# Two modulation chunks summed on TensorE, the first weights loaded earlier, and two blocks alternated by halves of the features

## The chip, the cores and the metric

One core of one Trainium2 chip. The metric is the device time in microseconds of one execution of the whole kernel, the median of the runs shown. Everything is float32; large matmuls are made of three float32r products.

## The reference, cut to what matters

A vector `c` of 1024 numbers gives a shift, a scale and a gate for each of the 1024 features; the normalized input (256 tokens by 1024 features) is scaled and shifted, and then multiplied by a wide input matrix, whose column blocks feed four attention branches a to d. A second, longer part of the model follows, which the change does not touch.

```python
mod = (jax.nn.silu(c) @ w_ada + b_ada)[:, None, :]
shift, scale, gate = jnp.split(mod, 3, axis=-1)
h = rms_norm(x, norm_g) * (1.0 + scale) + shift
(a_q, a_kv, a_g, a_z, b_q, b_k, b_v, b_z,
 c_q, c_k, c_v, c_z, d_q, d_k, d_v, d_z) = jnp.split(h @ w_in, IN_OFFSETS, axis=-1)
...
y_d = retention(heads(d_q), heads(d_k), heads(d_v))
...
yi = y.reshape(B, S, BRANCH_W) * jax.nn.silu(z)
term = jax.nn.sigmoid(h @ w_merge[i]) * (yi @ w_br[i])
...
return x + gate * (merged @ w_out)
```

## The kernel before

Each engine runs a program written out by hand, in its own order; an engine that waits for a semaphore holds up all that stands behind it on that engine.

**The stream of weights.** `weight_plan` (L105) lists all weights as chunks of 4 feature tiles (512 features) by up to 512 columns, 1 MB each. SyncE loads them in this order into four raw buffers (`sp_program`, L3004); chunk i may start when chunk i-4 is told `("weights low", i-4)`, which means that its raw form has been read for the last time. Two kinds of chunk come in this stream:

- Chunks of matrices that are multiplied. ScalarE rounds the chunk to its high part (`act_split`, L509), VectorE subtracts (`vec_split`, L519) to get the low part, and `pe_block` (L580) multiplies high and low parts. There are three pairs of buffers for the parts. I call these chunks split 0, 1, 2 and so on. A step of `pe_block` over 512 features is 48 matmuls of 256 columns where features are the output (`d_qk`, `c_qk`), 24 of 512 columns where tokens are (`pe_columns`: `d_vz`, `c_vz`).
- Chunks of `w_ada`, which gives the modulation. `vec_modulation` (L533 and L535) multiplies each of the 4 feature tiles by a number per partition and sums them on VectorE. For scale and shift, `pe_columns_of` (L829) then sums over the partitions with 4 matmuls of one column (8 matmul records in the profile), and `vec_first_columns` (L895 to L898) adds the bias. The gate's four chunks are each summed by `vec_split`, right behind the low part of the chunk that precedes them in the plan (L535).

**The start.** The plan begins with scale and shift of features 0 to 511 ("half 0"), then scale of half 1, then the first `w_in` chunk (`d_qk`, features 0 to 511), then shift of half 1, then the second `d_qk` chunk, then a gate chunk and `d_vz`. PE transposes the scaled x (`pe_turn_x`, L840), ScalarE applies scale and shift (L864) and rounds to the high operand (L868), VectorE makes the low operand (L906). Operand half n is ready when the last of these has run. `d_qk` step 0 needs half 0, step 1 needs half 1. The shift columns of half 1 are summed over the partitions within `d_qk` step 0, behind its 28th matmul, and operand half 1 is made after that.

**Later.** The blocks run on PE in the order `d_qk`, `d_vz`, `c_qk`, `c_vz`, `b_qk`, `b_vz`, `a_vz`, `a_qk`, and the small work of the four branches is put between their steps by `interleave`, by how many chunks each engine has passed. At split 11, branch d's retention output is normalized: VectorE (L1187 to L1195), GpSimd (L674, L676), VectorE again (L1198, L1028), and then PE transposes the result (L1036).

Of the kernel before, what the change touches and what calls it, by code (L numbers as in the profile page):

```python
# [14 lines left out]
P = 128  # L15
# [89 lines left out]
def weight_plan(w):  # L105
# [17 lines left out]
    first_in, shift = chunks(w_in, KT, [(W_D_Q, 512)]), modulation(ada, "shift", 1)  # L123
    plan.extend(modulation(ada, "scale", 0) + modulation(ada, "shift", 0) + modulation(ada, "scale", 1) + first_in[:1] + shift + first_in[1:])
    gate = modulation(ada, "gate", 0) + modulation(ada, "gate", 1)
    for block in ((W_D_V, 512), (W_C_Q, 512), (W_C_V, 512)):
        plan.append(gate.pop(0))
        add(w_in, [block])
    plan.append(gate.pop(0))
    add(w_in, [(W_B_Q, 384)], [(W_B_V, 384)])  # L130
    add(w_in, [(W_A_KV + 3 * HD, HD), (W_A_KV + 5 * HD, HD + 3 * NH + BW)], [(W_A_Q, BW + 3 * HD), (W_A_KV + 4 * HD, HD)])
    for i in ORDER:
# [358 lines left out]


def chain(*gens):
    for g in gens:
        yield from g
# [16 lines left out]

def vec_split(k, n, gate=True):

    if n < len(k.split):
        i, j = k.split[n], n % k.N_SPLIT
        raw, high, low = (chunk_view(k, t, i) for t in (k.w_raw[i % k.N_RAW], k.w_high[j], k.w_low[j]))
        k.vec.wait_ge(("weights high", i), ("weights", i), ("multiplied", n - k.N_SPLIT) if n >= k.N_SPLIT else None)
        k.vec.eng.tensor_tensor(low, raw, high.bitcast(F32), ALU.subtract).then_inc(*k.vec.tells("weights_low", ("weights low", i)))  # L519
        if gate and i + 1 < len(k.plan) and k.plan[i + 1][2] and k.plan[i + 1][2][0] == "gate":  # L520
            vec_modulation(k, *k.plan[i + 1][2])


def vec_modulation(k, name, n, first):

    V, i = k.vec, k.whole_weights[name, n, first]
    raw, total = chunk_view(k, k.w_raw[i % k.N_RAW], i), k.sums_of[name][:, n * CN:(n + 1) * CN]
    V.wait_ge("c silu", ("weights", i), "gate bias" if name == "gate" else None)
    for j in range(CK):
        number = k.c_silu[:, first + j:first + j + 1]  # L530
        V.wait_ge(V.last)
        if first + j == 0 and name != "gate":
            V.eng.tensor_scalar(total, raw[:, j, :], number, None, ALU.mult).then_inc(*V.tells("modulations"))  # L533
        else:
            V.eng.scalar_tensor_tensor(total, raw[:, j, :], number, total, ALU.mult, ALU.add).then_inc(  # L535
                *V.tells("modulations", (name, n), ("weights low", i)))


def act_chunk(k):

    i = k.act.chunk
    k.act.chunk += 1
    act_split(k, i + k.N_SPLIT - 1)


def vec_chunk(k):
    i = k.vec.chunk
    k.vec.chunk += 1
    vec_split(k, i + k.N_SPLIT - 1)

# [269 lines left out]


def pe_columns_of(k, name, n):

    key, at = ("columns", n), CK * ("scale", "shift").index(name)
    bank = k.product.take(key)
    k.pe.wait_ge((name, n), "common", None if at else k.product.before(key))
    for j in range(CK):
        c = (CK * n + j) * P
        mm = k.pe.eng.matmul(bank[:, at + j:at + j + 1], k.sums_of[name][:, c:c + P], k.ones[:, 0:1], start=at + j == 0, stop=True, skip_group_check=True)  # L829
    mm.then_inc(*k.pe.tells("columns", key))  # L830


# [11 lines left out]
def pe_condition(k):  # L844
    pe, tr = k.pe, k.pe.eng.transpose
    pe.wait_ge("common", "c row")
    tr(k.small.take("c")[:, 0:KT], k.c_row[:, :], k.ident[0:KT, 0:KT]).then_inc(*pe.tells("turned", "c turned"))
    pe.wait_ge("condition rows")
    tr(k.small.take("condition")[:, 0:3 * KT], k.cond_rows[:, :], k.ident[0:3 * KT, 0:3 * KT]).then_inc(*pe.tells("turned", "condition turned"))
    pe_columns_of(k, "scale", 0)  # L850
    pe_columns_of(k, "shift", 0)
    for n in range(2):
        pe_turn_x(k, n)
    pe_columns_of(k, "scale", 1)
    pe.ended("condition")


def act_first_half(k, n):
    A, columns = k.act, k.stat(("columns", n), 2 * CK)
    for b in range(2):  # L860
        for j in range(2):
            f = 2 * b + j
# [3 lines left out]
        at = slice(CK * n + 2 * b, CK * n + 2 * b + 2)  # L866
        A.wait_ge(A.last)
        A.eng.activation(k.H_first.high[:, at, :], k.whole[:, 2 * b:2 * b + 2, :], ACT.Copy).then_inc(*A.tells("operand_high", ("first high", n, b)))  # L868


def act_condition(k):
# [11 lines left out]
    act_first_half(k, 0)  # L883
    act_split(k, 1)
    act_first_half(k, 1)
    A.ended("condition")
# [3 lines left out]
def vec_first_columns(k, n):  # L890
    V, columns, ps = k.vec, k.stat(("columns", n), 2 * CK), k.product.of(("columns", n))
# [4 lines left out]
    V.eng.tensor_tensor(columns[:, CK:2 * CK], ps[:, CK:2 * CK], bias, ALU.add).then_inc(*V.tells("vec_steps", k.product.free(("columns", n))))  # L896
# [13 lines left out]
def vec_condition(k):  # L910
# [18 lines left out]
    V.ended("condition")  # L929
# [693 lines left out]
def act_branches(k):  # L1623
# [27 lines left out]
    def fill():  # L1651
        yield from act_qk(k, "d_qk", k.q_d, k.k_d, "d_qk")
        yield from act_vz(k, "d_vz", k.v_d, k.z["d"])
        yield from act_qk(k, "c_qk", k.q_c, k.k_c, "c_qk")
# [21 lines left out]
def vec_branches(k):  # L1676
# [3 lines left out]
    def fill():  # L1680
        yield from vec_chunks(k, 2)
        yield from vec_vz(k, "d_vz", BW, k.z["d"])
        yield from vec_chunks(k, 2)
# [1389 lines left out]
```

## Time and profile before

| | |
|---|---|
| median of 3 runs | 1157.37 us (1156.54 to 1158.16) |
| the profiled execution's own time | 1156.71 us |
| its span, first to last instruction | 1155.2 us |
| PE busy | 1116.3 us (97%) |
| DVE busy (VectorE) | 769.3 us (67%) |
| ACT busy (ScalarE) | 582.8 us (50%) |
| mean granted TensorE clock | 0.992 |
| first matmul of `d_qk` | 32.49 us |
| last matmul of `d_vz` ends, branch work begins | 63.14 us |

The span is 1.5 us shorter than the time of its own execution. PE is busy nearly everywhere but in the first 32 us, so what matters is when its first block starts, and how long PE waits after that. A granted clock of 1.00 in the profile is 2.4 GHz, 0.50 is 1.2 GHz.

### The profile page before, as it was taken

Reading aid. Unit: us, or ns where it says so; the run is one execution under the profiler, and the core shown is the slowest. Engines: PE = TensorE matmul, PEld = TensorE weight load, DVE = VectorE, ACT = ScalarE, POOL = GpSimd, SP = SyncE. Lnnn points to the kernel's source line nnn. Section 1 sums busy time; section 2 is a strip of 40 time slices with the busy share of each in tenths; the row PEclk is TensorE's granted clock in tenths of the full one; section 3 lists DMA queues with packets and bytes.
Section 4 is the critical chain, followed back from the end, with each engine's and each line's share of the span. In section 5 each row is a group of like instructions: output and inputs, shape, how many; then the busy total and the mean of one; then the engine's idle time right before and its main releaser. Section 6 shows DMA issues by size and latency. Waiting matters only on the chain.

```text
span 1155.2 us, 15556 instructions
## 1 busy us (share of the span) xinstructions
PE 1116.3 (97%) x6395; PEld 976.4 (85%) x6395; DVE 769.3 (67%) x1022; ACT 582.8 (50%) x830; POOL 49.3 (4%) x82
## 2 busy tenths in 40 slices
PE   2899999999999999999999999999999999999997
PEld 2789988888889987898988888788888989888886
DVE  6866655665787996745588765456876545788642
ACT  2547664444464764654544544446765545444441
POOL 3021000000010000000100000000011000000000
PEclk9999998999999999999999999999999999999999
DMA  9895343465546403543655555555345436555450
GB/s 350 307 315 167 114 144 128 158 224 165 195 141 204 140 1 109 186 143 123 175 182 180 185 184 180 189 181 176 111 157 171 146 109 201 177 189 182 152 176 37
DMA packets 105879, 195.10 MB, mean 169 GB/s; under 512 B 6105, under 2 KB 22641, under 8 KB 105808
## 3 DMA queue, kind: packets, MB, share of 16 engines
q1 hardware_dynamic: 103248, 187.51, 48.5%
q0 software_dynamic: 2560, 6.60, 2.1%
q8 instruction: 50, 0.82, 0.3%
q14 instruction: 21, 0.17, 0.0%
HBM read 193.04 MB, written 1.05 MB: 168 GB/s over the span
## 4 chain that ended last, share of the span: by engine, by line
PE 88%; DVE 4%; ACT 4%; DMA 2%; issue 1%; POOL 1%; SPq 0%; DVEq 0%; ACTq 0%; POOLq 0%
PE product L580 59%; PE product L614 5%; PE small L614 5%; PE small L2325 4%; PE product L616 3%; PE small L616 3%; ACT w_high L509 1%; DMA w_raw<-in_w_ada 1%; PE small L724 1%; PE small L1903 1%; PE small L1275 1%; DVE w_low L519 1%; DMA w_raw<-in_w_in 1%; PE small L1286 1%; PE small L1924 1%
## 5 line engine op out<-in xcount | busy, mean ns | idle before, releaser
L519 DVE TENSOR_TENSOR w_low<-w_raw,w_high 128x2048 fp32r<-128x2048 f32 (+3 forms) x172 | 377.6, 2198 | 219.6 <-ACT w_high L509 217.9
L509 ACT ACTIVATE w_high<-w_raw 128x2048 fp32r<-128x2048 f32 (+3 forms) x172 | 315.4, 1837 | 198.6 <-PE product L580 142.0
L580 PE MATMUL product<-w_high,H 128*128 128x512 f32 (+2 forms) x768 | 244.0, 392 | 0.2 <-DVE w_low L519 0.2
L580 PE MATMUL product<-H,w_high 128*128 128x256 f32 x1136 | 214.3, 288 | 5.6 <-DVE H L906 4.6
L580 PEld LDWEIGHTS product<-H,w_high 128*128 128x128 f32 x1136 | 181.8, 195 | 7.2 <-issue 6.3
L580 PEld LDWEIGHTS product<-w_high,H 128*128 128x128 f32 x768 | 144.8, 189 | 29.6 <-issue 1.2
L580 PE MATMUL product<-H,w_low 128*128 128x256 f32 x568 | 163.0, 287 | 0.0
L580 PE MATMUL product<-w_low,H 128*128 128x512 f32 (+2 forms) x384 | 149.3, 389 | 0.0
L580 PEld LDWEIGHTS product<-H,w_low 128*128 128x128 f32 x568 | 110.7, 195 | 0.3
L614 PE MATMUL product<-H,w_high 128*128 128x512 f32 x256 | 90.8, 399 | 0.0
L614 PE MATMUL small<-H,w_high 128*128 128x512 f32 x256 | 90.8, 399 | 0.0
L580 PEld LDWEIGHTS product<-w_low,H 128*128 128x128 f32 x384 | 72.8, 189 | 13.3 <-issue 0.2
L616 PE MATMUL product<-H,w_low 128*128 128x256 f32 x256 | 71.9, 281 | 0.0
L616 PE MATMUL small<-H,w_low 128*128 128x256 f32 x256 | 71.9, 281 | 0.0
L580 PE MATMUL product<-w_high,hidden_low 128*128 128x512 f32 x176 | 69.5, 395 | 0.0
L580 PE MATMUL product<-w_low,hidden_high 128*128 128x512 f32 x176 | 69.4, 395 | 0.0
L580 PE MATMUL product<-w_high,hidden_high 128*128 128x512 f32 x176 | 69.4, 395 | 0.0
L2482 DVE SCALAR_TENSOR_TENSOR conv_out<-conv_in,taps,conv_out 128x256 f32<-128x256 f32 x147 | 58.8, 489 | 0.0
L614 PEld LDWEIGHTS small<-H,w_high 128*128 128x128 f32 x256 | 48.1, 188 | 12.1
L614 PEld LDWEIGHTS product<-H,w_high 128*128 128x128 f32 x256 | 48.1, 188 | 12.0
L616 PEld LDWEIGHTS product<-H,w_low 128*128 128x128 f32 x256 | 48.4, 189 | 0.0
L616 PEld LDWEIGHTS small<-H,w_low 128*128 128x128 f32 x256 | 48.4, 189 | 0.0
(385 smaller groups left out, 1634.8 us busy)
## 6 DMA issues: line engine op xcount, KB each, us to landing
w_raw<-in_ffn_w_gate SPq DMA_DIRECT2D x20, 1024.0 KB, 5.1
w_raw<-in_ffn_w_up SPq DMA_DIRECT2D x20, 1024.0 KB, 5.2
w_raw<-in_ffn_w_down SPq DMA_DIRECT2D x20, 1024.0 KB, 5.1
w_raw<-in_w_merge SPq DMA_DIRECT2D x16, 1024.0 KB, 5.1
w_raw<-in_w_ada SPq DMA_DIRECT2D x12, 1024.0 KB, 7.9
w_raw<-in_w_in SPq DMA_DIRECT2D x8, 1024.0 KB, 6.3
w_raw<-in_mem_w_k SPq DMA_DIRECT2D x8, 1024.0 KB, 5.1
w_raw<-in_conv_w_pw SPq DMA_DIRECT2D x16, 512.0 KB, 4.7
```

Source lines behind the costliest of these rows:

```text
L509: k.act.eng.activation(chunk_view(k, k.w_high[j], i), chunk_view(k, k.w_raw[i % k.N_RAW], i), ACT.Copy).then_inc(*k.act.tells("weights_hig ...
L519: k.vec.eng.tensor_tensor(low, raw, high.bitcast(F32), ALU.subtract).then_inc(*k.vec.tells("weights_low", ("weights low", i)))
L580: mm = pe.eng.matmul(bank[:, off:off + wide], a, r, start=b not in started, stop=True, skip_group_check=True)
L614: pe.eng.matmul(bank[:, :].rearrange("p (i n) -> p i n", n=S), high[:, j, column], x.parts[:, :, first + j, :], start=first + j == 0, stop ...
L616: mm = pe.eng.matmul(bank[:, 0:S], low[:, j, column], x.high[:, first + j, :], start=False, stop=True, skip_group_check=True)
L724: tr = k.pe.eng.transpose(bank[:, j * S + t * P:j * S + (t + 1) * P], k.X[:, t, c:c + P], k.ident)
L1275: mm = pe.eng.matmul(scores[:, i * nk:(i + 1) * nk], q[:, h, t * P:(t + 1) * P], kk_of(h)[:, 0:nk], start=i == 0, stop=True, skip_group_ch ...
L1286: mm = pe.eng.matmul(mixed[:, i * HD:(i + 1) * HD], p[:, b * P:(b + 1) * P], v_of(h, j), start=b == 0, stop=True, skip_group_check=True)
L1903: mm = pe.eng.matmul(bank[:, t * S:(t + 1) * S], k.q_mem[:, kt, t * P:(t + 1) * P], k.mem_keys[:, kt, :], start=t == 0 and j == 0, stop=Tr ...
L1924: mm = pe.eng.matmul(bank[:, f * S:(f + 1) * S], k.mem_values[:, j, c:c + P], p[:, j * S:(j + 1) * S], start=f == 0 and j == 0, stop=True, ...
L2325: mm = pe.eng.matmul(bank[:, 0:S], slot[:, i, :], k.conv_in[:, f, tap:tap + S], start=tap in (0, VEC_TAPS) and i == 0, stop=tap == TAPS - 1)
L2482: V.eng.scalar_tensor_tensor(y[:, f, :], src, wt, y[:, f, :], ALU.mult, ALU.add).then_inc(*V.tells("taps_vec", ("conv out", f)))
```

## The change

The plan's head is put in another order. Before, with the splits numbered: scale 0, shift 0 (two chunks each), scale 1 (two), `d_qk` (split 0), shift 1 (two), `d_qk` (1), gate, `d_vz` (2, 3), gate, `c_qk` (4, 5), gate, `c_vz` (6, 7), gate, `b_qk` (8, 9), `b_vz` (10, 11), `a_vz` (12, 13). After: scale 0, shift 0, `d_qk` (0), scale 1 (two), `d_vz` (1), shift 1 (first), `d_qk` (2), shift 1 (second), `d_vz` (3), `c_qk` (4, 5), gate, `c_vz` (6, 7), `b_qk` (8), gate, `b_qk` (9), `b_vz` (10, 11), gate, `a_vz` (12, 13), gate.

The first chunk of scale 1 and the second of shift 1 are no longer summed by VectorE: `pe_direct_columns` multiplies the raw weights by `c_silu` on PE, 16 matmuls of one column each. The columns of half 1 go to another PSUM ring. VectorE takes one of the two pairs of tiles of half 1 from ScalarE (`vec_last_whole`). `d_qk` and `d_vz` alternate: step 0 of each, then step 1 of each; the columns of scale 1 are summed within `d_qk` step 0, those of shift 1 within `d_vz` step 0.

```diff
-    plan.extend(modulation(ada, "scale", 0) + modulation(ada, "shift", 0) + modulation(ada, "scale", 1) + first_in[:1] + shift + first_in[1:])
+    plan.extend(modulation(ada, "scale", 0) + modulation(ada, "shift", 0) + first_in[:1] + modulation(ada, "scale", 1))
...
+    plan.extend(d_vz[:1] + shift[:1] + first_in[1:] + shift[1:])
+    a_vz = chunks(w_in, KT, [(W_A_KV + 3 * HD, HD), (W_A_KV + 5 * HD, HD + 3 * NH + BW)])
+    for part in (d_vz[1:] + c_qk, c_vz + b_qk[:1], b_qk[1:] + b_vz, a_vz):
+        plan.extend(part + [gate.pop(0)])
...
+def alternate(*gens):
+
+    gens = list(gens)
+    while gens:
+        for gen in list(gens):
+            said = next(gen, "end")
...
+            if said == "end":
+                gens.remove(gen)
+            else:
+                yield said
...
+DIRECT = [("scale", 1, 0), ("shift", 1, CK)]
+
+
+def columns_ring(k, n):
+    return k.small if n else k.product
...
+def pe_direct_columns(k, name, n, first):
+
+    key, at, ring, i = ("columns", n), CK * ("scale", "shift").index(name), columns_ring(k, n), k.whole_weights[name, n, first]
+    raw, bank = chunk_view(k, k.w_raw[i % k.N_RAW], i), ring.take(key)
+    k.pe.wait_ge("c silu", ("weights", i), None if at else ring.before(key))
+    for f in range(CK):
+        for j in range(CK):
+            mm = k.pe.eng.matmul(bank[:, at + f:at + f + 1], raw[:, j, f * P:(f + 1) * P], k.c_silu[:, first + j:first + j + 1],
+                                 start=(at, f, j) == (0, 0, 0), stop=True, skip_group_check=True)
+    mm.then_inc(*k.pe.tells("columns", key, ("weights low", i)))
...
     pe_columns_of(k, "scale", 0)
+    pe_turn_x(k, 0)
     pe_columns_of(k, "shift", 0)
-    for n in range(2):
-        pe_turn_x(k, n)
-    pe_columns_of(k, "scale", 1)
+    pe_turn_x(k, 1)
+    pe_direct_columns(k, "scale", 1, 0)
     pe.ended("condition")
...
+def vec_last_whole(k):
+
+    V, columns, key = k.vec, k.stat(("columns", 1), 2 * CK), ("x", 1, 1)
+    V.wait_ge(V.last, ("x turned", 1, 1))
+    for j in range(2):
+        f = 2 + j
+        V.eng.tensor_scalar(k.whole[:, f, :], k.small.of(key)[:, S * j:S * (j + 1)], columns[:, f:f + 1], columns[:, CK + f:CK + f + 1],
+                            ALU.mult, ALU.add).then_inc(*V.tells("last_whole", "last whole", k.small.free(key)))
...
-    vec_modulation(k, "scale", 1, 0)
     vec_first_columns(k, 0)
-    vec_modulation(k, "scale", 1, CK)
     vec_split(k, 0)
     vec_first_low(k, 0)
-    for first in range(0, KT, CK):
-        vec_modulation(k, "shift", 1, first)
+    vec_modulation(k, "scale", 1, CK)
+    vec_split(k, 1)
+    vec_modulation(k, "shift", 1, 0)
+    vec_split(k, 2)
     vec_first_columns(k, 1)
-    vec_split(k, 1, False)
+    vec_last_whole(k)
     vec_first_low(k, 1)
-    vec_modulation(k, "gate", 0, 0)
...
+    def last_columns():
+        pe_direct_columns(k, "shift", 1, CK)
+        pe_columns_of(k, "shift", 1)
+
     def fill():
-        yield from pe_block(k, "d_qk", k.H_first, KT, FEATURES, inside={(0, 28): lambda: pe_columns_of(k, "shift", 1)})
-        yield from pe_columns(k, "d_vz", k.H_first, KT)
+        yield from alternate(pe_block(k, "d_qk", k.H_first, KT, FEATURES, inside={(0, 28): lambda: pe_columns_of(k, "scale", 1)}),
+                             pe_columns(k, "d_vz", k.H_first, KT, inside={(0, 10): last_columns}))
```

## Rows read from the trace of the kernel before

**Rows 1.** The page: busy time of each engine, and the granted clock in 40 slices:

```profile
PE 1116.3 (97%) x6395; PEld 976.4 (85%) x6395; DVE 769.3 (67%) x1022; ACT 582.8 (50%) x830; POOL 49.3 (4%) x82
...
PEclk9999998999999999999999999999999999999999
```

**Rows 2.** Windows: length, then each engine's busy time, PEclk, DMA share, GB/s:

```profile
32.49:63.14 30.65, 28.21 (x152) 25.58 (x152) 25.16 (x27) 14.94 (x15) 1.13 (x2) 0.94 0.90 307
...
110.94:1150.00 1039.06, 1031.48 (x5891) 898.66 (x5891) 691.82 (x922) 527.82 (x758) 26.19 (x44) 1.00 0.47 157
```

**Rows 3.** Waits of PE: waited for, us in total, times, longest:

```profile
PE product L829 <- DVE gain L535: 12.4, 3, 6.1
...
PE product L580 <- DVE H L906: 4.6, 2, 2.3
...
PE small L1036 <- DVE y L1028: 0.9, 1, 0.9
```

**Rows 4.** Timeline of PE: start, us, line, operation, idle before and its releaser:

```profile
21.54 1.87 PE L829 MATMUL product<-common,gain 128*128 128x1 f32 x8 [6.14 <-DVE gain L535]
...
23.27 3.65 PE L840 MATMUL small<-common,scaled_x 128*128 128x128 f32 x16
...
32.49 0.55 PE L580 MATMUL product<-H,w_high 128*128 128x256 f32 x1 [2.35 <-DVE H L906]
...
38.58 1.05 PE L829 MATMUL product<-common,gain 128*128 128x1 f32 x8
...
44.40 0.36 PE L580 MATMUL product<-H,w_high 128*128 128x256 f32 x1 [2.27 <-DVE H L906]
...
52.04 0.50 PE L580 MATMUL product<-w_high,H 128*128 128x512 f32 x1 [0.16 <-DVE w_low L519]
```

**Rows 5.** Windows of PE alone: length, busy (instructions), granted clock, DMA:

```profile
32.49:38.41 5.92, 5.92 (x28) 1.00 0.96 330
...
38.41:42.00 3.59, 3.59 (x30) 1.00 0.99 322
...
45.24:48.65 3.41, 3.41 (x18) 0.50 0.51 188
```

**Rows 6.** SyncE's queue at 10 and 18 us: issues, and us to landing:

```profile
10.29 0.37 SPq L3014 DMA_DIRECT2D w_raw<-in_w_ada  x1
...
w_raw<-in_w_ada SPq DMA_DIRECT2D x1, 1024.0 KB, 10.6
...
w_raw<-in_w_in SPq DMA_DIRECT2D x1, 1024.0 KB, 8.3
```

**Rows 7.** Timelines of ScalarE and VectorE around the first operand half:

```profile
28.38 1.00 ACT L864 ACTIVATE whole<-small,stats 128x256 f32<-128x256 f32 x2
...
29.42 0.63 ACT L868 ACTIVATE H<-whole 128x512 fp32r<-128x512 f32 x1
...
28.51 2.29 DVE L519 TENSOR_TENSOR w_low<-w_raw,w_high 128x2048 fp32r<-128x2048 f32 x1 [0.28 <-ACT w_high L509]
...
31.66 0.69 DVE L906 TENSOR_TENSOR H<-whole,H 128x512 fp32r<-128x512 f32 x1 [0.26 <-ACT H L868]
```

**Rows 8.** PE at 185 us, timeline, then the window behind it:

```profile
184.79 3.70 PE L1380 MATMUL small<-cmp_t,cmp_w 128*128 128x16 f32 x32
...
188.60:191.04 2.44, 2.44 (x8) 0.50 0.25 93
```

**Rows 9.** Timelines of VectorE and PE where branch d's output is turned:

```profile
75.23 3.11 DVE L535 SCALAR_TENSOR_TENSOR gate<-w_raw,stats,gate 128x512 f32<-128x512 f32 x4
...
105.60 1.75 DVE L519 TENSOR_TENSOR w_low<-w_raw,w_high 128x1536 fp32r<-128x1536 f32 x1
...
107.73 0.55 DVE L1256 TENSOR_TENSOR merged<-merged,small 128x384 f32<-128x384 f32 x1
...
109.46 0.69 DVE L1198 TENSOR_TENSOR y<-y,stats 128x512 f32<-128x512 f32 x1 [1.18 <-POOL stats L676]
...
110.94 0.66 PE L1036 MATMUL small<-common,y 128*128 128x128 f32 x4 [0.88 <-DVE y L1028]
```

More of the change, by code:

```diff
@@ L123, in weight_plan @@
     first_in, shift = chunks(w_in, KT, [(W_D_Q, 512)]), modulation(ada, "shift", 1)
-    plan.extend(modulation(ada, "scale", 0) + modulation(ada, "shift", 0) + modulation(ada, "scale", 1) + first_in[:1] + shift + first_in[1:])
+    plan.extend(modulation(ada, "scale", 0) + modulation(ada, "shift", 0) + first_in[:1] + modulation(ada, "scale", 1))
     gate = modulation(ada, "gate", 0) + modulation(ada, "gate", 1)
[L126 to L131, printed above, removed]
+    d_vz, c_qk, c_vz, b_qk, b_vz = (chunks(w_in, KT, [block]) for block in ((W_D_V, 512), (W_C_Q, 512), (W_C_V, 512), (W_B_Q, 384), (W_B_V, 384)))
+    plan.extend(d_vz[:1] + shift[:1] + first_in[1:] + shift[1:])
+    a_vz = chunks(w_in, KT, [(W_A_KV + 3 * HD, HD), (W_A_KV + 5 * HD, HD + 3 * NH + BW)])
+    for part in (d_vz[1:] + c_qk, c_vz + b_qk[:1], b_qk[1:] + b_vz, a_vz):
+        plan.extend(part + [gate.pop(0)])
+    add(w_in, [(W_A_Q, BW + 3 * HD), (W_A_KV + 4 * HD, HD)])
     for i in ORDER:
@@ L490, in drain @@
         pass
+def alternate(*gens):
[3 more added lines that the diff above has]
+            said = next(gen, "end")
+            while said == "piece":
+                yield said
+                said = next(gen, "end")
+            if said == "end":
+                gens.remove(gen)
+            else:
+                yield said
 def chain(*gens):
@@ L510, in act_split, with vec_split @@
             *k.act.tells("weights_high", ("weights high", i)))
-def vec_split(k, n, gate=True):
+def vec_split(k, n):
     if n < len(k.split):
@@ L519, in vec_split @@
         k.vec.eng.tensor_tensor(low, raw, high.bitcast(F32), ALU.subtract).then_inc(*k.vec.tells("weights_low", ("weights low", i)))
-        if gate and i + 1 < len(k.plan) and k.plan[i + 1][2] and k.plan[i + 1][2][0] == "gate":
+        if i + 1 < len(k.plan) and k.plan[i + 1][2] and k.plan[i + 1][2][0] == "gate":
             vec_modulation(k, *k.plan[i + 1][2])
@@ L531, in vec_modulation @@
         V.wait_ge(V.last)
-        if first + j == 0 and name != "gate":
+        if j == 0 and name != "gate" and (first == 0 or (name, n, 0) in DIRECT):
             V.eng.tensor_scalar(total, raw[:, j, :], number, None, ALU.mult).then_inc(*V.tells("modulations"))
@@ L542, in act_chunk @@
     k.act.chunk += 1
-    act_split(k, i + k.N_SPLIT - 1)
+    if i:
+        act_split(k, i + k.N_SPLIT - 1)
 def vec_chunk(k):
@@ L548, in vec_chunk @@
     k.vec.chunk += 1
-    vec_split(k, i + k.N_SPLIT - 1)
+    if i:
+        vec_split(k, i + k.N_SPLIT - 1)
 def pe_block(k, key, x, tiles, items, order=None, inside={}, early={}):
@@ L819, in pool_condition @@
     g.wait_ge(*k.all_ended("condition"))
+DIRECT = [("scale", 1, 0), ("shift", 1, CK)]
+def columns_ring(k, n):
+    return k.small if n else k.product
 def pe_columns_of(k, name, n):
-    key, at = ("columns", n), CK * ("scale", "shift").index(name)
-    bank = k.product.take(key)
-    k.pe.wait_ge((name, n), "common", None if at else k.product.before(key))
+    key, at, ring = ("columns", n), CK * ("scale", "shift").index(name), columns_ring(k, n)
+    bank = ring.take(key)
+    k.pe.wait_ge((name, n), "common", None if at else ring.before(key))
     for j in range(CK):
         c = (CK * n + j) * P
-        mm = k.pe.eng.matmul(bank[:, at + j:at + j + 1], k.sums_of[name][:, c:c + P], k.ones[:, 0:1], start=at + j == 0, stop=True, skip_group_check=True)
+        mm = k.pe.eng.matmul(bank[:, at + j:at + j + 1], k.sums_of[name][:, c:c + P], k.ones[:, 0:1], start=(at, j, n) == (0, 0, 0), stop=True,
+                             skip_group_check=True)
     mm.then_inc(*k.pe.tells("columns", key))
+def pe_direct_columns(k, name, n, first):
[7 more added lines that the diff above has]
+    mm.then_inc(*k.pe.tells("columns", key, ("weights low", i)))
 def pe_turn_x(k, n):
@@ L860, in act_first_half @@
     for b in range(2):
-        for j in range(2):
+        for j in range(0 if n and b else 2):
             f = 2 * b + j
@@ L866, in act_first_half @@
         at = slice(CK * n + 2 * b, CK * n + 2 * b + 2)
-        A.wait_ge(A.last)
+        A.wait_ge("last whole" if n and b else A.last)
         A.eng.activation(k.H_first.high[:, at, :], k.whole[:, 2 * b:2 * b + 2, :], ACT.Copy).then_inc(*A.tells("operand_high", ("first high", n, b)))
@@ L884, in act_condition @@
     act_split(k, 1)
+    act_split(k, 2)
     act_first_half(k, 1)
@@ L890, in vec_first_columns @@
 def vec_first_columns(k, n):
-    V, columns, ps = k.vec, k.stat(("columns", n), 2 * CK), k.product.of(("columns", n))
+    V, columns, ring = k.vec, k.stat(("columns", n), 2 * CK), columns_ring(k, n)
+    ps = ring.of(("columns", n))
     at = slice(CK * n, CK * (n + 1))
@@ L895, in vec_first_columns @@
     V.eng.tensor_tensor(columns[:, 0:CK], ps[:, 0:CK], scale, ALU.add).then_inc(*V.tells("vec_steps"))
-    V.eng.tensor_tensor(columns[:, CK:2 * CK], ps[:, CK:2 * CK], bias, ALU.add).then_inc(*V.tells("vec_steps", k.product.free(("columns", n))))
+    V.eng.tensor_tensor(columns[:, CK:2 * CK], ps[:, CK:2 * CK], bias, ALU.add).then_inc(*V.tells("vec_steps", ring.free(("columns", n))))
     V.wait_ge(V.last)
     V.eng.scalar_tensor_tensor(columns[:, 0:CK], columns[:, 0:CK], 1.0, gain, ALU.add, ALU.mult).then_inc(*V.tells("columns_copied", ("columns copied", n)))
+def vec_last_whole(k):
[5 more added lines that the diff above has]
+                            ALU.mult, ALU.add).then_inc(*V.tells("last_whole", "last whole", k.small.free(key)))
 def vec_first_low(k, n):
@@ L1651, in fill @@
     def fill():
-        yield from act_qk(k, "d_qk", k.q_d, k.k_d, "d_qk")
-        yield from act_vz(k, "d_vz", k.v_d, k.z["d"])
+        yield from alternate(act_qk(k, "d_qk", k.q_d, k.k_d, "d_qk"), act_vz(k, "d_vz", k.v_d, k.z["d"]))
         yield from act_qk(k, "c_qk", k.q_c, k.k_c, "c_qk")
@@ L1680, in fill @@
     def fill():
-        yield from vec_chunks(k, 2)
-        yield from vec_vz(k, "d_vz", BW, k.z["d"])
+        yield from alternate(vec_chunks(k, 2), vec_vz(k, "d_vz", BW, k.z["d"]))
         yield from vec_chunks(k, 2)
```

## The prediction

> **What bounds the kernel now.** I read the page first. PE is busy for 1116.3 of 1155.2 us, and the granted clock is near 1.00 in all slices but one [rows 1]. The windows and the table of PE's waits then tell where PE is not busy. Of its 39 us of idle time, 24 fall before the first matmul of `d_qk` at 32.49 us; behind 110.94 us it is busy for 1031.48 of 1039.06 us [rows 2, 3]. So the rest of the kernel is bound by PE, and a shift of PE near the start reaches the end unchanged. Two waits lie where the change works: `d_qk` step 1 waits 2.27 us for the low operand of half 1, and at 110 us PE waits 0.88 us for branch d's gated output [rows 3, 4, 9].
>
> PE's clock matters too. From 32.49 to 38.41 us PE issued 28 matmuls of 256 columns in 5.92 us, 0.211 us each: that is 1.2 GHz, although the row says 1.00. From 38.41 us on, 30 matmuls (among them the 8 short ones of the columns) took 3.59 us, the pace of 2.4 GHz [rows 5]. Before the lower stretch PE had transposed and made one-column matmuls. 0.84 us after the wait of 2.27 us the granted clock fell to 0.50 for 3.41 us, in which PE did half its work: such a fall costs 1.7 us [rows 4, 5].
>
> **The change, part by part.**
>
> *Start of `d_qk`.* The first `w_in` chunk goes from place seven of the stream to place five. It takes over the place of a chunk issued at 10.29 us that landed 10.6 us later, at 20.9 us; before, it was issued at 18.3 and landed at 26.6 [rows 6]. ScalarE is free then, so its high part (1.9 us) is made by 22.8 us. The shift columns of half 0 are summed at 21.54 us as before, and end at 23.4 us [rows 4]. Their three small vector steps end near 24.0 us. ScalarE then makes operand half 0: 1.0 + 0.6 + 1.0 + 0.6 us with overlap is 3.25 us, to 27.3 us; the last low part takes 0.7 us, to 28.05 us [rows 7]. VectorE's split 0 (2.29 us) fits beside it, 24.1 to 26.4 us. The data of `d_qk` are thus ready 4.4 us earlier than at 32.49 us.
>
> But PE is not. Behind the shift columns stand 8 transposes (half of 3.65 us, to 25.1 us), and then `pe_direct_columns` for scale 1: 16 float32 matmuls, 32 records. The same form, 128x128 weights by one column, took 1.87 us for 8 records at this stage, with 1.73 us from its start to the next instruction, so 0.216 us a record [rows 4]. 32 records are 6.9 us, at most 7.5. `d_qk` starts at about 25.15 + 6.9 = 32.05 us, against 32.49: a gain of 0.4 us, and at worst a loss of 0.1. The earlier landing is nearly all eaten by PE's own queue.
>
> *`d_qk` and `d_vz`.* The matmuls are the same in number: 96 of 256 columns and 48 of 512. Added is the second direct sum (shift 1), now at the full clock. Its price is in the trace: 32 records with 128x128 weights and 16 columns took 3.70 us [rows 8]; with the change of work around it I take 3.75. Before, one sum over partitions (8 records, 0.96 us from start to start) ran within `d_qk` and one stood ahead of it, while data were missing; now both stand within: 0.96 us more [rows 4]. Removed is the wait of 2.27 us and the 0.16 us before `d_vz` [rows 4].
>
> Is operand half 1 in time? With these durations `d_qk` step 0 ends at 41.75 us, 10 matmuls of `d_vz` at 0.227 us reach 44.1, the direct sum 47.9, the columns 48.85 us. From there the vector steps take 0.45 us, ScalarE's first pair and its high part 1.7 us, the second high part 0.65 us (VectorE has made that pair meanwhile), the low part 0.7 us: ready at about 52.4 us, 3.55 us later [rows 7]. What hides it is the 14 matmuls of `d_vz` left: 3.2 us at 2.4 GHz, about 5 where the clock falls. I take no wait; without the fall it is 0.4 us. The weights are no limit: split 1 is ready at 33.5 us, split 2 at 41.6, split 3 (ScalarE and VectorE come to it when half 1 is done) at 56.8 against a need at 59.4. `d_qk`'s heads, now copied by ScalarE behind step 2 instead of step 1, are done near 62, before the scores at 65.
>
> *The clock there.* The fall of 3.41 us behind the wait goes with the wait. In its place stand 40 records of one column, 4.7 us. The 32 records of 16 columns at 184.79 us were followed by a fall at 188.60 us to 0.50 [rows 8]. I take one fall again, so no difference.
>
> The Trainium skill (TensorE: Matmul & The Clock Gate, Part 1) says that activity releases the throttle, which the row of 38.41 us agrees with; it would let PE's unbroken work from 21.5 us on count. By it the first block would start warm, which is the third rival below; [rows 4, 5] speak against it, as 5.4 us of columns and transposes without a gap did not bring the upper level.
>
> Sum of this part: -0.4 - 2.4 + 3.75 + 0.96 = **+1.9 us** at the end of `d_vz`, 65.0 us instead of 63.14.
>
> *VectorE and the gate chunks.* The two chunks taken off VectorE (about 3 us each) were under PE's other work or under data that are no longer waited for: nothing further. The gate's four sums of 3.11 us stood behind operand half 1 and splits 3, 5 and 7; they now stand behind splits 5, 8, 11 and 13 [rows 9]. Behind 5, 8 and 13 VectorE has idle time or its readers have slack. Split 11 is the row at 105.60 us [rows 9]. Behind it stand two steps of branch c (to 108.3 us), then 1.18 us of idle time for GpSimd's root, then L1198 at 109.46 us and L1028, and PE's transposes at 110.94 us wait for the latter. With 3.11 us put behind split 11, the two steps of branch c end at 111.4 us, and L1198 starts 3.11 - 1.18 = 1.93 us later; with one handover between instructions, 2.0. PE's wait grows from 0.88 to 2.9 us: **+2.0 us**. What waits behind it on PE is `b_vz`'s second step, and all of the rest. ScalarE's part of branch c moves by 3.2 us, of which 2.0 are PE's own, and split 12 is then ready 3.8 us before its need; no second wait. Lower bound 0, if VectorE is further ahead than before; upper bound 3.1, the whole sum.
>
> *The clock there.* Around that wait PE has 1.6 us of short matmuls before it and 0.4 us of transposes behind it, 4.9 us in all without large matmuls. Before, the same place with 0.88 us of wait kept 1.00. The 2.27 us wait in front of `d_qk` step 1 brought a fall [rows 4, 5]. The cost is 0 or 1.7 us. The new wait is nearer to the second row, but where in time it comes is open: I put in **+0.9 us**.
>
> **Sum.** 1.9 + 2.0 + 0.9 = 4.8 us. Against the profiled execution's own 1156.71 us (1.5 us more than its span) that is 1161.5; its time is 0.66 us under the median of 1157.37 us, to which I add the sum: **1162.2 us**.
>
> **Rivals.**
> 1. *The gate sum behind split 11 is hidden.* VectorE has two modulation sums less to do, and could be ahead of its times of before. Against it: at 105 us its work is chained to PE through ScalarE and not to its load at 50 us. Only the first 1.9 us remain: 1159.3 us.
> 2. *The direct sums cost more.* 0.234 us a record at the start (+0.6), a wait of 0.4 for half 1, and the full fall behind the second wait, or a longer one (the fall at 188.60 lasted beyond 191 us, as short matmuls followed [rows 8]): +1.7 more on the 4.8, 1165 us or above.
> 3. *Not slower: the direct sum holds the clock up.* PE has no gap from 21.5 us on. If the clock reaches its upper level half-way through the first direct sum, the rest of it takes 1.9 us instead of 3.6 (-1.7), the first 28 matmuls 3.4 instead of 6.1 us (-2.7), and no fall comes within `d_vz` (-1.7, less 0.5 of waiting for half 1). 1.9 - 5.6 = -3.7 us for the start; with the wait at 110 us 1155.7, without it 1153.7 us. It decides once the first matmuls of `d_qk` are 0.12 us apart. For it: PE works without a break. Against it: [rows 8], where the same form let the clock fall.
> 4. *It comes out even.* The early landing and the removed wait together weigh the direct sums, because the clock's stretches fall otherwise: 1157.4 us.
>
> **Chances.** Forecast (both waits as worked out, 1160.5 to 1164.0 us) 0.50; rival 1 0.17; rival 2 0.10; rival 3 0.16; rival 4 0.07. 0.2% is 2.3 us, about what a measurement of this kernel tells from no change. Slower by more than that, above 1159.7: the forecast, rival 2 and part of rival 1, 0.62. Faster, below 1155.1: half of rival 3 and a little more, 0.12. Same: the rest, 0.26. The range for 8 in 10 goes from 1155.3 us, with part of rival 3 in it, to 1165.0 us.
>
> **What would show it.** Right: the first `w_in` chunk lands near 21 us; 32 records of the direct sum from 25 to 32 us, right in front of the first L580 matmul, which waits for no operand; no wait for H in `d_qk` step 1; another 32 records in about 3.7 us near 44 us, with a stretch of granted clock 0.50 behind them; `d_vz` ends near 65 us; PE's wait for L1028 is near 2.9 us. Wrong: a direct record of 0.12 us at the start; `d_qk` starting near 28 to 30 us; the L1028 wait unchanged; or a new wait of PE for `w_low`, `queries_keys` or a DMA.

## The result and the profile after

| | before | changed |
|---|---|---|
| median | 1157.76 us (1156.54 to 1159.50, 4 runs) | 1163.67 us (1161.92 to 1164.43, 4 runs) |
| ratio | | 1.0047 (95% interval 1.0034 to 1.0060) |
| span of the profiled execution | 1155.2 us | 1160.6 us |

By the medians the change made the kernel 5.9 us slower, by the ratio 5.4 us, with an interval from 3.9 to 7.0 us. Forecast were 4.8 us (1162.2 us against 1157.4) and a range of 1155.3 to 1165.0 us.

The start first. This is the timeline of PE in the changed kernel, to be held against [rows 4]:

```profile
21.55 1.87 PE L853 MATMUL product<-common,gain 128*128 128x1 f32 x8 [1.11 <-DVE gain L550]
...
23.28 1.95 PE L877 MATMUL small<-common,scaled_x 128*128 128x128 f32 x8
...
25.21 6.96 PE L865 MATMUL small<-stats,w_raw 128*128 128x1 f32 x32
...
32.04 0.56 PE L597 MATMUL product<-H,w_high 128*128 128x256 f32 x1
...
37.89 0.95 PE L853 MATMUL small<-common,gain 128*128 128x1 f32 x8
...
43.46 3.62 PE L865 MATMUL small<-stats,w_raw 128*128 128x1 f32 x32
...
46.95 1.11 PE L853 MATMUL small<-common,gain 128*128 128x1 f32 x8
...
52.72 0.28 PE L597 MATMUL product<-H,w_high 128*128 128x256 f32 x1
...
64.03 0.70 PE L1051 MATMUL small<-queries_keys 64*128 64x256 f32 x2
```

The 32 records of the first direct sum stand from 25.21 to 32.04 us, right in front of the first matmul of `d_qk`, and that matmul has no idle time before it: it waits for PE itself. It starts 0.45 us earlier than before. The operand it needs was there long ago, as ScalarE and then VectorE show (timelines of both, against [rows 7]):

```profile
20.90 1.91 ACT L524 ACTIVATE w_high<-w_raw 128x2048 fp32r<-128x2048 f32 x1 [2.49 <-DMA w_raw<-in_w_in]
...
26.67 0.63 ACT L905 ACTIVATE H<-whole 128x512 fp32r<-128x512 f32 x1
```

```profile
27.33 0.69 DVE L955 TENSOR_TENSOR H<-whole,H 128x512 fp32r<-128x512 f32 x1 [0.57 <-ACT H L905]
```

The first `w_in` chunk's high part begins at 20.90 us, and the last low part of half 0 ends at 28.0 us. PE came 4.0 us later. Further down in PE's timeline, the second direct sum takes 3.49 us from its start to the next instruction (43.46 to 46.95) and the columns 0.97 us; `d_qk` step 1 (52.72) does not wait; branch work begins at 64.03 us against 63.14.

Now the place at 110 us, VectorE above and PE below, against [rows 9]:

```profile
106.49 1.75 DVE L534 TENSOR_TENSOR w_low<-w_raw,w_high 128x1536 fp32r<-128x1536 f32 x1
...
108.35 3.14 DVE L550 SCALAR_TENSOR_TENSOR gate<-w_raw,stats,gate 128x512 f32<-128x512 f32 x4
...
111.41 0.55 DVE L1308 TENSOR_TENSOR merged<-merged,first_constants 128x384 f32<-128x384 f32 x1
...
113.19 0.69 DVE L1076 TENSOR_TENSOR y<-y,z_d 128x512 f32<-128x512 f32 x1
```

```profile
112.02 0.43 PE L1059 MATMUL small<-v_c,merged 128*128 128x64 f32 x2 [2.53 <-DVE merged L1308]
...
112.97 1.22 PE L1051 MATMUL small<-queries_keys 64*128 64x256 f32 x2
...
114.55 1.11 PE L1084 MATMUL small<-common,y 128*128 128x128 f32 x4
```

The gate's sum stands behind split 11 (L534 at 106.49) and pushes branch c's step L1308 to 111.41 us. PE's small matmul L1059 needs that step and waits 2.53 us. Branch d's output (L1076) is ready at 113.9 us, and PE's transposes of it (L1084, at 114.55) no longer wait. So the wait is there with nearly the forecast's size, but at an earlier instruction of PE, branch c's mix, and not at branch d's transposes.

The third view is windows of PE alone (length, busy time, granted clock, DMA), laid on the stretches where the clock stood low:

```profile
32.04:37.52 5.48, 5.48 (x27) 1.00 0.78 254
...
47.76:51.18 3.42, 3.42 (x10) 0.50 0.84 264
...
112.62:119.44 6.82, 6.82 (x24) 0.50 1.01 337
```

The first 27 matmuls of `d_qk` run at the 1.2 GHz pace although the row says 1.00, as in [rows 5]. The clock falls to 0.50 behind the second direct sum for 3.4 us, and at 112.62 us, 0.6 us behind the end of the new wait, for 6.8 us. The second of these costs 3.4 us, where I had put in 0.9.

When the starts of the same PE instruction in both traces are subtracted, the changed kernel is 0.89 us late at 63.14 us and still so at 104 us, 3.6 us late at the mix behind the new wait, and 5.87 us late at the next small matmuls of branch c (115.62 us before). Between there and 890 us this does not change (5.43 us behind that). Both losses lie before 122 us, and the rest carries them to the end. The second adds up: 1.65 us more of waiting and 3.4 us of clock are 5.05 us, against 4.98 from branch work to there.

### The profile page after: what moved, and what is told of

Same layout as the page of the kernel before. It is cut to its first block, busy times and chain, and to the rows that moved or that the text cites. A ratio compares the mean times of both kernels' runs of the same rounds, so it can differ in the third digit from the quotient of the medians.

```text
span 1160.6 us, 15674 instructions
## 1 busy us (share of the span) xinstructions
PE 1128.5 (97%) x6459; PEld 988.1 (85%) x6459; DVE 764.3 (66%) x1016; ACT 581.4 (50%) x828; POOL 49.0 (4%) x82
## 3 DMA queue, kind: packets, MB, share of 16 engines
HBM read 193.04 MB, written 1.05 MB: 167 GB/s over the span
## 4 chain that ended last, share of the span: by engine, by line
PE 91%; DVE 4%; ACT 3%; DMA 1%; issue 1%; SPq 0%; POOL 0%; DVEq 0%; ACTq 0%; POOLq 0%
PE product L597 61%; PE product L631 5%; PE small L631 5%; PE small L2375 4%; PE product L633 3%; PE small L633 3%; DMA w_raw<-in_w_ada 1%; ACT w_high L524 1%; PE small L741 1%; PE small L1953 1%; PE small L865 1%; PE small L1323 1%; DVE w_low L534 1%; PE small L656 1%; PE small L1334 1%
## 5 line engine op out<-in xcount | busy, mean ns | idle before, releaser
L534 DVE TENSOR_TENSOR w_low<-w_raw,w_high 128x2048 fp32r<-128x2048 f32 (+3 forms) x172 | 377.5, 2197 | 226.8 <-ACT w_high L524 224.8
L631 PEld LDWEIGHTS product<-H,w_high 128*128 128x128 f32 x256 | 48.1, 188 | 11.9
```

Source lines behind the costliest of these rows:

```text
L631: pe.eng.matmul(bank[:, :].rearrange("p (i n) -> p i n", n=S), high[:, j, column], x.parts[:, :, first + j, :], start=first + j == 0, stop ...
```

## The experiments

The experiments were timed in three sets (1 to 4, 5 to 7, 8 and 9), each on one chip beside the kernel before, so kernels of different sets are compared by their ratios to it. Two numbers besides the median are used. **Start** is the time from PE's transposes at 23.27 us [rows 4], or what answers to them, to branch work (63.14 us before), so that a late landing of the first loads is left out: 39.9 us before. It comes from one trace of each kernel. **Lost clock** is one minus the mean granted clock, times the span, averaged over all executions of a kernel. Every execution has some: 10.3 us before on average, and 6.9 to 16.2 us in 34 executions; a single trace shows one draw.

| kernel | median, us | ratio (95%) | start | lost clock | mean time less lost clock |
|---|---|---|---|---|---|
| before | 1157.4 | | 39.9 | 10.3 | 1147.7 |
| changed | 1163.7 | 1.0047 | 40.8 | 12.5 | 1150.9 |
| changed, again | 1164.5 | 1.0049 (1.0036 to 1.0062) | 41.3 | 14.2 | 1149.9 |
| gate sums moved | 1161.2 | 1.0026 (1.0017 to 1.0035) | 41.7 | 12.9 | 1148.1 |
| before, gate sums late | 1161.3 | 1.0025 (1.0015 to 1.0035) | 37.8 | 12.3 | 1148.7 |
| shift chunk on VectorE | 1160.7 | 1.0020 (1.0011 to 1.0030) | 38.5 | 11.0 | 1149.4 |
| both | 1155.5 | 0.9983 (0.9972 to 0.9993) | 38.4 | 8.4 | 1147.7 |
| both, no direct sum | 1155.7 | 0.9980 (0.9968 to 0.9992) | 38.1 | 10.5 | 1145.1 |
| both, shift chunk first | 1156.7 | 0.9987 (0.9975 to 0.9998) | 39.3 | 9.4 | 1147.1 |
| no direct sum, shift first | 1158.3 | 1.0000 (0.9990 to 1.0010) | 39.4 | 11.9 | 1146.3 |
| direct sum spread | 1159.3 | 1.0005 (0.9993 to 1.0016) | 40.0 | 9.7 | 1149.4 |

Lost clock is not the time that the lower level costs, and the last column is not the time without it. The trace of the kernel before has its last low stretch from 1151 us on, where PE has no work left. The low pace of the first matmuls of `d_qk` is not in it either, as the row there says 1.00 [rows 5]. Over the 34 executions of the kernel before, taking the lost clock off makes the spread larger and not smaller (standard deviation 2.2 us instead of 1.35). The column is shown, but no reading below rests on it.

**Start** has a draw of its own. In the seven traces that have the first direct sum, `d_qk` began 8.75 to 8.76 us behind the start of the transposes each time, but its step 0, the same work, ended 16.8 to 17.9 us behind them, because the pace doubled sooner or later. So a difference of up to 1.1 us in start can be this alone.

### 1. The gate sums moved

```diff
-    for part in (d_vz[1:] + c_qk, c_vz + b_qk[:1], b_qk[1:] + b_vz, a_vz):
+    for part in (d_vz[1:] + c_qk, c_vz, b_qk, b_vz + a_vz):
```

> The changed kernel with one thing moved: the gate sums stand behind splits 5, 7, 9 and 13 instead of 5, 8, 11 and 13. In the traces PE ran 0.89 us later than before at the end of d_vz, and 5.87 us later behind branch d's turn at 110 us. My theory: the 3.11 us sum behind split 11 makes nearly all of the 5 us between (a longer wait of PE and the fall of the clock that it brings). Then this kernel is 4.5 to 5 us faster than the changed one, about 1158.7 us, with PE's wait there back at 0.9 us and a granted clock of 1.00 from 105 to 125 us. Rival: VectorE's chain through ScalarE and GpSimd is late in any case, and the gate sum only fills a wait; then no more than 1 us comes back.

Measured: 1161.2 us; by the ratios 2.4 us less than the changed kernel, and 2.7 less than its second timing, where 4.5 to 5 had been expected. PE's waits from 60 to 150 us, and windows of PE:

```profile
PE small L1084 <- DVE y L1076: 0.9, 1, 0.9
```

```profile
47.15:53.97 6.82, 6.82 (x22) 0.50 0.64 219
...
100.00:130.00 30.00, 29.11 (x183) 1.00 0.72 231
```

The wait is back at 0.9 us and the clock stays up from 100 to 130 us, so the mechanism at 110 us is as stated, and the rival (VectorE's chain is late in any case) is out. In this trace the whole 5 us came back: between branch work and 121.5 us PE makes up 5.0 us on the first trace of the changed kernel, and 3.4 us on its second trace. The medians show only half of the 5 us, with an uncertainty of 1.8. Part of the difference is that the fall behind the direct sum lasted 6.8 us here and not 3.4; over ten executions the lost clock is 12.9 us, no less than the changed kernel's 12.5. I had taken the clock's share from one trace as if it were fixed.

### 2. The late gate sums alone, in the kernel before

```diff
-    for block in ((W_D_V, 512), (W_C_Q, 512), (W_C_V, 512)):
-        plan.append(gate.pop(0))
...
+    for part in (d_vz + c_qk, c_vz + b_qk[:1], b_qk[1:] + b_vz, a_vz):
+        plan.extend(part + [gate.pop(0)])
...
     vec_first_low(k, 1)
-    vec_modulation(k, "gate", 0, 0)
```

> The kernel before with one part of the change alone: the gate sums behind splits 5, 8, 11 and 13. My theory: 3 to 5 us slower than before, 1161 to 1163 us, by the same wait for VectorE near 111 us and the clock behind it, while d_vz ends at 63.1 us as before or 0.2 us earlier. Rival (the start sets everything): within 1 us of before.

Measured: 1161.3 us, 3.9 us slower than before (2.9 by the ratio), as the theory says, with nothing else of the change in it. Its wait of PE, and three rows of its PE timeline:

```profile
PE small L1009 <- DVE merged L1258: 2.5, 1, 2.5
```

```profile
24.37 3.58 PE L839 MATMUL small<-common,scaled_x 128*128 128x128 f32 x16
...
29.38 1.05 PE L828 MATMUL product<-common,gain 128*128 128x1 f32 x8 [1.44 <-DVE gain L534]
...
62.16 0.70 PE L1001 MATMUL small<-queries_keys 64*128 64x256 f32 x2
```

The wait is the same 2.5 us, at the same small matmul. The start is even shorter than before by 2.1 us. In this trace the clock had reached its upper level by the columns at 29.38 us, behind nothing but short matmuls, transposes and 1.4 us of waiting (they took 1.05 us instead of 1.87), and it did not fall around the 2.28 us wait for the second operand half. It did fall at 31.2 us, within the 3.0 us wait in front of `d_qk`, for 6.8 us. The edit touches nothing there, and the lost clock over its 11 executions is 12.3 us against 10.3 before, so I take the shorter start as a draw of this one execution.

### 3. The second direct sum undone

```diff
-DIRECT = [("scale", 1, 0), ("shift", 1, CK)]
+DIRECT = [("scale", 1, 0)]
...
     vec_modulation(k, "shift", 1, 0)
+    vec_modulation(k, "shift", 1, CK)
     vec_split(k, 2)
...
     def last_columns():
-        pe_direct_columns(k, "shift", 1, CK)
         pe_columns_of(k, "shift", 1)
```

> The changed kernel with the second direct sum undone: VectorE sums the second chunk of shift 1 as before (3.1 us, ahead of split 2), PE makes only its 8 column records in d_vz step 0. My theory: PE loses 3.5 us of work and the fall of the clock behind it (1.7 us), but operand half 1, now behind VectorE's split 2, is then what d_qk step 1 waits for, 1 to 2 us; d_vz ends near 60.3 us instead of 64.0, and the kernel is 3 to 4 us faster than the changed one, about 1160 us, as the wait near 111 us stays. Rival: the direct sum was hidden behind operand half 1; then d_vz ends at 63.5 us or later and the time is that of the changed kernel.

Measured: 1160.7 us; by the ratios 3.1 us less than the changed kernel (3.4 less than its second timing). PE's timeline:

```profile
45.30 1.05 PE L853 MATMUL small<-common,gain 128*128 128x1 f32 x8 [1.75 <-DVE gain L550]
...
62.54 0.70 PE L1052 MATMUL small<-queries_keys 64*128 64x256 f32 x2
```

The columns now wait 1.75 us for VectorE's sum, and this wait, not one for the operand half, is what is set against the 3.5 us saved. The fall of the clock, which I had expected to go as well, stayed: the trace has one of 3.4 us from 46.6 us on, behind this wait and the columns. Branch work begins 2.3 us sooner after the transposes, of which 0.9 us is the earlier doubling of the pace in `d_qk` step 0 and 1.4 us the edit. The direct sum was no hidden work, but `d_vz` ended 2.2 us later than the 60.3 us expected.

### 4. Both edits

> Both edits: gate sums behind splits 5, 7, 9 and 13, and the shift chunk on VectorE. If the two costs are separate stretches of one chain on PE, the gains add: 8 to 9 us faster than the changed kernel, about 1155 us, and 2 to 3 us faster than before. If either gain only takes up slack of the other, it stays at 1157 or above.

Measured: 1155.5 us, by the ratios 7.4 us less than the changed kernel, and 2.0 less than before (ratio 0.9983, 0.9972 to 0.9993). PE's timeline:

```profile
24.77 1.95 PE L877 MATMUL small<-common,scaled_x 128*128 128x128 f32 x8
...
45.87 1.05 PE L853 MATMUL small<-common,gain 128*128 128x1 f32 x8 [1.79 <-DVE gain L550]
...
51.74 0.36 PE L597 MATMUL product<-H,w_high 128*128 128x256 f32 x1
...
63.12 0.70 PE L1052 MATMUL small<-queries_keys 64*128 64x256 f32 x2
```

The gains add within the noise: 2.4 and 3.1 us alone, 7.4 together, and the 1.9 us between have an uncertainty of 2.4 by the intervals. This version keeps the early first chunk and the alternation. Its interval lies below that of the changed kernel and just below 1, so it is also faster than the kernel before, by 0.2%.

### 5. No direct sum at all

```diff
-DIRECT = [("scale", 1, 0)]
+DIRECT = []
...
-    pe_direct_columns(k, "scale", 1, 0)
     pe.ended("condition")
...
+    vec_modulation(k, "scale", 1, 0)
     vec_modulation(k, "scale", 1, CK)
```

> The kernel of both edits (gate sums behind 5, 7, 9, 13; shift chunk on VectorE) with the first direct sum undone as well: VectorE sums the first chunk of scale 1 (3.1 us) behind operand half 0, and nothing stands on PE between the transposes and d_qk. My theory: the direct sum of 6.9 us at 1.2 GHz held d_qk back by 4 us, so d_qk starts 3.5 to 4.4 us earlier against the last transposes; but the chain to operand half 1 on VectorE (four sums, splits 1 and 2) then ends PE's d_vz step 0 with a wait of 2 to 4 us, and d_vz ends 1 to 2 us earlier than with both edits: 1153.5 to 1155 us. Rival: VectorE with one more sum is the bound of the start; then d_vz ends 1 us or more later than with both edits, 1156 us or more.

Measured: 1155.7 us, the time of both edits, and 0.7 us above the range expected. PE's timeline:

```profile
24.29 1.95 PE L877 MATMUL small<-common,scaled_x 128*128 128x128 f32 x8
...
29.19 0.55 PE L597 MATMUL product<-H,w_high 128*128 128x256 f32 x1 [2.95 <-DVE H L954]
...
43.65 1.87 PE L853 MATMUL small<-common,gain 128*128 128x1 f32 x8 [2.54 <-DVE gain L550]
...
51.04 0.28 PE L597 MATMUL product<-H,w_high 128*128 128x256 f32 x1
...
62.35 0.70 PE L1052 MATMUL small<-queries_keys 64*128 64x256 f32 x2
```

`d_qk` starts 4.9 us behind the transposes instead of 8.8: the first direct sum had held it back by 3.9 us. What is left in front of `d_qk` is a wait of 2.95 us for operand half 0. Later PE waits 0.64 us for the scale sum and 2.54 us for the shift sum (1.79 with both edits); for operand half 1 it does not wait. The clock is low from 43.7 to 50.5 us in this trace (the columns at 43.65 take 1.87 us), 3.4 us longer than with both edits. Against the transposes the lead of 3.9 us is 1.7 at the shift columns and 0.3 at branch work. Neither theory nor rival has it wholly: PE's earlier start is real, and in this trace it goes to the waits for VectorE's sums and to the lower clock behind them.

### 6 and 7. The shift chunk loaded first

```diff
-    plan.extend(d_vz[:1] + shift[:1] + first_in[1:] + shift[1:])
+    plan.extend(d_vz[:1] + shift + first_in[1:])
...
-    vec_split(k, 2)
     vec_first_columns(k, 1)
+    vec_split(k, 2)
```

The seventh makes these edits in the fifth's kernel, and puts `last_columns` behind the 20th matmul: `inside={(0, 20): last_columns}`.

> The kernel of both edits with the second shift chunk loaded in front of d_qk's second chunk, and the columns of half 1 computed before split 2. My theory: operand half 1 hangs on the landing of that shift chunk and on split 2 in front of it; it gets ready about 2 us earlier, PE's wait of 1.8 us for the sum goes, and a wait for the operand half of up to 1.3 us comes: 1 to 2 us faster than with both edits, 1153.5 to 1154.5 us. Rival: PE's work, not the operand half, sets the end of d_vz: no more than 0.5 us.

> Both of the last two edits at once, no direct sum and the shift chunk first, and the columns behind the 20th matmul of d_vz step 0 instead of the 10th. My theory: d_qk starts 4 us earlier, operand half 1 is ready about 1 us earlier than with the shift chunk first alone, PE waits 3 to 4 us for it: 0.5 to 1.5 us faster than that kernel, 1152.5 to 1153.5 us, unless the wait brings a longer stretch of the lower clock. Rival: PE's longer wait lowers the clock for more than it gains: 1154.5 us or more.

Measured: 1156.7 us and 1158.3 us; both expectations missed, each was to be faster than the kernel it started from. PE's timelines, the sixth and then the seventh:

```profile
23.64 1.95 PE L877 MATMUL small<-common,scaled_x 128*128 128x128 f32 x8
...
50.07 0.35 PE L597 MATMUL product<-H,w_high 128*128 128x256 f32 x1 [1.99 <-DVE H L955]
...
62.94 0.70 PE L1052 MATMUL small<-queries_keys 64*128 64x256 f32 x2
```

```profile
23.58 1.95 PE L877 MATMUL small<-common,scaled_x 128*128 128x128 f32 x8
...
28.48 0.55 PE L597 MATMUL product<-H,w_high 128*128 128x256 f32 x1 [2.95 <-DVE H L954]
...
49.31 0.55 PE L597 MATMUL product<-H,w_high 128*128 128x256 f32 x1 [4.30 <-DVE H L954]
...
63.02 0.70 PE L1052 MATMUL small<-queries_keys 64*128 64x256 f32 x2
```

The wait for the sum is gone or nearly so (0.27 us in the seventh), but one for the operand half has come, 1.99 us and 4.30 us. `d_qk` step 1 does start sooner behind the transposes: 26.4 us instead of 27.0 in the fourth experiment, and 25.7 instead of 26.8 in the fifth. But it then takes 7.3 and 8.2 us instead of 5.8, since the clock falls behind the wait, for 3.4 us in the sixth and for 6.8 us in the seventh, where the fall begins within the wait. So in the traces the clock takes back what the earlier operand half gives, which is the mechanism of the seventh's rival. Its size is not shown by them: branch work begins at the same time in both, and the seventh's further 1.6 us come at 210 us, where a fall lasted 6.8 us instead of 3.4. Over all executions the lost clock is 11.9 us against 9.4. The sixth's start is 0.9 us longer than the fourth's, and that is there at the end of `d_qk` step 0 already, before the edit acts.

### 8. The second direct sum spread

```diff
-                             pe_columns(k, "d_vz", k.H_first, KT, inside={(0, 10): last_columns}))
+                             pe_columns(k, "d_vz", k.H_first, KT, inside={(0, 2): direct(0), (0, 5): direct(1), (0, 8): direct(2), (0, 11): last_columns}))
```

Each `direct(f)` makes the 4 matmuls (8 records) of one column of the sum; the last stands in `last_columns`. The gate sums are as in the first experiment.

> The changed kernel with the gate sums moved (behind splits 5, 7, 9, 13) and the second direct sum cut into four pieces of 8 records, each behind three more matmuls of d_vz step 0, the last with the columns behind the 11th. The work is the same. My theory: the fall of the clock at 47 us follows from 4.5 us without a large matmul, so with the pieces apart it does not come: 1.7 us or more faster than with the gate sums moved alone, 1158 to 1159.5 us, and no granted clock of 0.50 between 40 and 55 us. Rival: the share of one-column matmuls brings it, not their being in one piece; then the fall stays and the time is 1160.5 to 1162 us.

Measured: 1159.3 us beside a before of 1158.5; by the ratios (1.0005 and 1.0026) 2.4 us less than the first experiment, as expected. PE's timeline, and a window of PE:

```profile
41.99 0.95 PE L865 MATMUL small<-stats,w_raw 128*128 128x1 f32 x8
...
43.58 0.94 PE L865 MATMUL small<-stats,w_raw 128*128 128x1 f32 x8
...
52.40 0.35 PE L597 MATMUL product<-H,w_high 128*128 128x256 f32 x1 [0.69 <-DVE H L955]
...
63.79 0.70 PE L1051 MATMUL small<-queries_keys 64*128 64x256 f32 x2
```

```profile
40.00:56.00 16.00, 15.31 (x109) 1.00 0.82 287
```

The same 32 records, with three large matmuls between each eight, and the granted clock is 1.00 from 40 to 56 us. The lost clock falls from 12.9 to 9.7 us. So the fall at 47 us goes with one-column work in one piece, not with its amount. The trace has the place, and the medians and the lost clock the gain; other orders of the pieces were not tried. A wait of 0.69 us for the operand half appears, as the columns end later.

### 9. The changed kernel again

> The changed kernel as it is, once more, beside the run above: for its median from more executions and for a second trace. Theory: 1162.5 to 1163.7 us; a fall of the clock behind the direct sum and one behind the wait near 112 us again, but each may last 3.4 or 6.8 us. If the stretches of the lower clock come out otherwise than in the first trace while the waits of PE stay the same, the difference between single executions is the clock's.

Measured: 1164.5 us (a ratio of 1.0049), 0.8 us above the range expected, beside a kernel before that was 1.1 us above its usual median. PE's timeline at the start, and two windows of PE:

```profile
42.78 4.16 PE L865 MATMUL small<-stats,w_raw 128*128 128x1 f32 x32
...
46.80 1.85 PE L853 MATMUL small<-common,gain 128*128 128x1 f32 x8
...
64.99 0.70 PE L1051 MATMUL small<-queries_keys 64*128 64x256 f32 x2
```

```profile
45.69:52.52 6.83, 6.83 (x25) 0.50 0.79 269
...
113.96:117.37 3.41, 3.41 (x12) 0.50 1.02 386
```

The program and PE's wait of 2.53 us are the same; the clock is not. Here the fall behind the direct sum began within it (its 32 records take 4.02 us) and lasted 6.8 us, the one at 114 us 3.4 us. In the first trace it was 3.4 and 6.8. At branch work PE is 1.85 us late against [rows 4]; the first trace had 0.89. But 0.4 us of this were there at the transposes: the start is 41.3 us, 1.4 more than before. At 121.5 us this trace is 0.6 us ahead of the first, and at the end 2.6 us behind it. All of that comes between 194 and 234 us, where it had low stretches of 6.8, 6.8 and 3.4 us and the first trace 6.8 and 3.4.

## Why the prediction was right, and where not

- **Start of `d_qk`.** Forecast: data ready at 28.05 us, PE at 32.05. Measured: 28.0 and 32.04. The landing gained 4.4 us and the direct sum in front of the block took it. Without that sum (experiment 5) `d_qk` starts 3.9 us earlier, which did not make the kernel faster. (PE's idle time ahead of `d_qk` before was 22.8 us and not the 24 of the prediction; nothing hangs on it.)
- **Second direct sum.** Forecast 3.75 us from the rows with 16 columns; measured 3.49, and 4.02 where the clock fell within it. The columns: 0.96 forecast, 0.97 measured.
- **Operand half 1.** Forecast: ready near 52.4 us, no wait as long as the clock falls. No wait in either trace; with the clock held up (experiment 8) it is 0.69 us.
- **Sum of the start.** Forecast +1.9 us; measured from the transposes on, +0.9 and +1.4 us in two traces. That is 0.5 to 1.0 us less than forecast, within what the doubling of the pace in `d_qk` step 0 moves from trace to trace.
- **The gate sum behind split 11.** Right in place and nearly in size (2.0 forecast, 1.65 more wait measured: 2.53 against 0.88). Wrong was which instruction of PE waits. The prediction moved the two steps of branch c with the sum, but followed only L1028 to its reader, whose wait was to be 2.9 us and is gone; the first of the two steps feeds the mix that stands on PE before branch d's transposes, and it was the one waited for. Experiment 2 gives this part alone, with its clock: 3.9 us by the medians, 2.9 by the ratio.
- **The clock behind that wait.** The term that was mis-sized. I put in 0.9 us, half of one fall of 3.4 us. It came in both traces, for 6.8 and 3.4 us, which cost 3.4 and 1.7 us. The whole forecast was 1.1 us too low, and this term alone was 0.8 to 2.5 us too small; that the sum came nearer than its term is in part luck, as the start was forecast 0.5 to 1.0 us too high.
- **Rivals.** The even outcome (rival 4) lies outside the interval, and the 1165 us of rival 2 were not reached, though its longer fall behind the second wait came in the first trace. The hidden gate sum (rival 1) is excluded by the same wait of 2.5 us in four traces (the changed kernel's two, experiments 2 and 3). The direct sum holding the clock up (rival 3) is excluded for the changed kernel: in both traces the first matmuls of `d_qk` were at the lower pace, and a fall came behind the second sum or within it. The Trainium skill (TensorE: Matmul & The Clock Gate, Part 4) says that the full clock does not engage for PE's transposes. The trace of experiment 2 does not agree: its columns at 29.38 us, with nothing but transposes and 1.4 us of waiting between them and the shift columns at the lower pace, took 1.05 us.

How much of the 5.9 us is clock the runs do not fix. In the two traces the start is worth 0.9 and 1.4 us, the longer wait behind split 11 1.65 us in both, and the fall behind that wait 3.4 and 1.7 us. The lost clock is 2.2 to 3.8 us more than before, but it can't be taken off the time. What brings each single fall was not tested, but for the one at 47 us (experiment 8); the falls between 185 and 235 us, behind all that the change reorders, differ between traces by as much as the edits gain (10.2 us of low clock in the first trace, 17.1 in the second). That the alternation alone pays was not tried.

## What to carry to other kernels

Work moved to the engine that bounds the kernel is not free because data are missing there before the move: here the data came 4 us earlier and the moved sum filled all of it, and a second sum among work that did not wait cost 3 us. Taking the first sum off again gained nothing, as PE then waited for VectorE. When small sums are put elsewhere in a hand-written order, look up every reader on the bounding engine of what stands behind them, not only the one that waits today. In this kernel it paid to put short matmuls apart and between large ones: with the same 32 records in four pieces it was 2.4 us faster, and had 3.2 us less lost clock, than with them in one. And a saving of 1 to 2 us cannot be read from one trace of each kernel, when the falls of the clock move by as much.

## What the runs showed of the hardware

The lower clock came in stretches of 3.4 or 6.8 us, once of 10.2, and the same program had them at other places or of other lengths from one execution to the next: 1161.9 to 1164.8 us for the changed kernel, 1155.2 to 1161.3 us for the one before. A 2.27 us wait was followed by a fall in [rows 4, 5], while in the trace of experiment 2 the wait at the same place was not. At the start the pace of the matmuls doubled sooner in some traces than in others (the same step ended 16.8 to 17.9 us behind the transposes), and the granted clock read 1.00 throughout, so there the clock has to be read from the distance of the matmuls. And float32 matmuls of one column with 128x128 weights took 0.213 to 0.216 us a record at the lower pace and 0.109 us at the upper one; with 16 columns behind weights of the same size it was 0.116 us [rows 8], so between 1 and 16 columns their number hardly changes what such a matmul costs.
